# Moving the last layer's weights and first rows behind the cache pages of the last two sample batches

## What is computed

```
k_past = cache_k[page_table]          # 8 batches x 8 pages x (128 positions, 8 heads x 128)
v_past = cache_v[page_table]
s = q k^T * SCALE - slope * dist      # two components per head
p = softmax(s);  a = p[0] - lam * p[1]
o = a v                               # the sample rows' attention output

def diff_layer(...):                  # the last layer, prompt rows and sample rows alike
    o = rmsnorm(o, subln_g) * (1.0 - lambda_init)     # per head
    y = (o * silu(z)) @ w_out
    return x + y
y = rmsnorm(x, norm_f_g)
```

## Time and profile before

| | |
|---|---|
| median of 3 runs | 3050.28 us (3046.14 to 3050.70) |
| the profiled execution's own time | 3047.47 us |
| its span | 3045.8 us |
| mean granted TensorE clock | 0.989 of full speed |
| PE busy | 2953.3 us (97%) |
| sample batches, first key transpose to the last layer's first one | 2656 to 2818 us |

### The profile page before, as it was taken

How to read it: one execution, slowest core, us unless ns; L and a number is a source line. 1 busy time by engine, 2 the same in 40 slices (tenths; PEclk the granted TensorE clock), 3 DMA queues, 4 the chain that set the end, 5 groups by cost and what they waited for, 6 DMA issues and landing times. The chain is left out here.

```text
span 3045.8 us, 45887 instructions
## 1 busy us (share of the span) xinstructions
PE 2953.3 (97%) x17416; PEld 2481.7 (81%) x17416; DVE 1583.7 (52%) x2678; ACT 1268.9 (42%) x2236; POOL 135.4 (4%) x171
## 2 busy tenths in 40 slices
PE   8999999999989999899999999989999999988998
PEld 7888888889968888788888888879999999855786
DVE  3456555554532111443443433368888888644654
ACT  4443434442221101353433432257777777633422
POOL 0000000000000000000000000100000000021321
PEclk9999999999999999999999999989999999999999
DMA  7433443344344221455555455662444444399453
GB/s 259 148 137 103 141 142 124 115 147 148 119 131 154 96 97 69 155 197 187 190 186 190 158 175 184 178 158 63 103 110 103 105 108 100 121 417 407 166 181 104
DMA packets 271991, 470.33 MB, mean 154 GB/s; under 512 B 23785, under 2 KB 124633, under 8 KB 265529
## 3 DMA queue, kind: packets, MB, share of 16 engines
q1 hardware_dynamic: 269761, 467.73, 47.6%
q0 software_dynamic: 2048, 0.14, 0.0%
HBM read 357.19 MB, written 111.34 MB: 154 GB/s over the span
## 5 line engine op out<-in xcount | busy, mean ns | idle before, releaser
L1800 ACT ACTIVATE attn_scores<-attn_scores,attn_lowest 128x1024 f32<-128x1024 f32 (+15 forms) x256 | 306.8, 1203 | 10.6 <-DVE attn_lowest L1853 10.6
L1853 DVE CUSTOM_DVE_ANT_0 attn_scores<-attn_s,region_early 128x1024 f32<-128x1024 f32 (+7 forms) x256 | 216.6, 856 | 105.8 <-PE attn_s L1741 72.6
L238 PE MATMUL pool_acc<-pool_odd_x_hi,pool_wh 128*128 128x512 f32 (+1 forms) x640 | 223.2, 349 | 0.0
L240 PE MATMUL pool_acc<-pool_odd_x_hi,pool_wl 128*128 128x512 f32 (+1 forms) x640 | 222.9, 348 | 0.0
L239 PE MATMUL pool_acc<-pool_odd_x_lo,pool_wh 128*128 128x512 f32 (+1 forms) x640 | 222.9, 348 | 0.0
L238 PE MATMUL outa_acc<-outa_w_hi,outa_g_hi 128*128 128x512 f32 x512 | 201.3, 393 | 10.8 <-DVE outa_w_lo L1053 9.6
L239 PE MATMUL outa_acc<-outa_w_lo,outa_g_hi 128*128 128x512 f32 x512 | 200.1, 391 | 0.0
L238 PE MATMUL pool_acc<-even_x,pool_wh 128*128 128x512 f32 x512 | 200.1, 391 | 0.0
L240 PE MATMUL outa_acc<-outa_w_hi,outa_g_lo 128*128 128x512 f32 x512 | 199.9, 391 | 0.0
L240 PE MATMUL pool_acc<-even_x,pool_wl 128*128 128x512 f32 x512 | 199.3, 389 | 0.0
L239 PE MATMUL pool_acc<-even_x,pool_wh 128*128 128x512 f32 x512 | 199.2, 389 | 0.0
(11 more groups left out here) (282 smaller groups left out, 6668.3 us busy)
## 6 DMA issues: line engine op xcount, KB each, us to landing
pool_wz<-in_w_in_a SPq DMA_DIRECT2D x18, 2048.0 KB, 8.3
pool_wu<-w_mix SPq DMA_DIRECT2D x16, 2048.0 KB, 8.0
region_early<-in_w_kv SPq DMA_DIRECT2D x16, 2048.0 KB, 9.3
region_early<-in_w_in_b SPq DMA_DIRECT2D x16, 2048.0 KB, 8.9
hold_kq<-in_cache_k SPq DMA_DIRECT2D x64, 512.0 KB, 9.9
region_early<-in_cache_v SPq DMA_DIRECT2D x64, 512.0 KB, 9.9
region_early<-gatedT SPq DMA_DIRECT2D x16, 1024.0 KB, 5.5
gatedT<-pool_gates SPq DMA_DIRECT2D x48, 256.0 KB, 2.2
```

The lines of the kernel that those rows point to most:

```text
L238: pe.matmul(out, ah, bh, start=first, stop=False)
L240: return pe.matmul(out, al, bh, start=False, stop=last)
L1800: act.activation(part, part, ACT.Exp, scale=-1.0, bias=low[s][:, x:x + 1], accum_out=sums[s][:, i:i + 1]).then_inc(expd, 1)
L1853: dve.tensor_tensor_reduce(sc[s][:, c, a0:a0 + n], s_ps[idx % 2][:, 0:n], bias[h % 2][:, b0:b0 + n], -SCALE, low[s][:, x - 2:x - 1] if x > ...
```

## The change

The transfers that the last layer needs first are split in two groups. Before, all of them (o, z and x1 of blocks 0 and 1, the weights in four transfers of 1 MB, and the final gain, 7.5 MB together) are issued right after k(1). After, o and z of block 0 and the weights (5 MB) are issued after v(6), and o and z of block 1, x1 of both blocks and the gain (2.5 MB) after v(7). To place the first group, the last turn of SP's loop over batches is written out. On POOL, `gate(0)` moves behind the stores of batches 0 to 5, and `gate(1)` behind the store of batch 6. The streams of PE, ACT and DVE are unchanged.

```
             load_v(0, True)
             load_k(1)
-            last.first_loads(sp)
-            with sp.Fori(2, NB) as b:
+            with sp.Fori(2, NB - 1) as b:
                 load_k(b)
                 load_v(b - 1)
+            load_k(NB - 1)
+            load_v(NB - 2)
+            last.first_loads(sp)
             load_v(NB - 1)
+            last.second_loads(sp)
             last.sync(sp, sample_stored)
...
             pool.sem_inc(o_stored, FREE)
+            with pool.Fori(0, LB - 1) as b:
+                store(b)
             gate(0, 0)
+            store(LB - 1)
             gate(1, 1)
-            with pool.Fori(0, LB) as b:
-                store(b)
             gate(2, 0)
             gate(3, 1)
             store(LB)
...
     def first_loads(self, sp):
         wv = self.D["w_out_b"][0].rearrange("(k p) n -> p k n", p=P)
-        for b in range(2):
-            self.load_oz(sp, b, b)
-            self.load_x1(sp, b, b)
+        self.load_oz(sp, 0, 0)
         for j in range(self.KC // 2):
             sp.dma_start(self.w[:, 2 * j:2 * j + 2, :], wv[:, 2 * j:2 * j + 2, :]).then_inc(self.w_sem[j], 16)
+
+    def second_loads(self, sp):
+        self.load_oz(sp, 1, 1)
+        self.load_x1(sp, 0, 0)
+        self.load_x1(sp, 1, 1)
         sp.dma_start(self.gf[:, :], self.D["norm_f_g"].partition_broadcast(P)).then_inc(self.gf_in, 16)
```

## The result

The changed kernel is slower: 3056.58 us (median of 17 runs, 3053.90 to 3064.52) against 3050.28 us. The ratio of the runs to those of the kernel before is 1.0025, 95% interval 1.0019 to 1.0032, so 0.25% or 7.6 us slower by the ratio (6.3 us by the medians). Its profiled execution took 3055.36 us with a span of 3053.7 us, 7.9 us more than the span of before. The runs scatter with the clock: six of the 17 took 3059.5 to 3064.5 us at a mean granted clock of 0.983 to 0.986, the other eleven 3053.9 to 3057.6 us at 0.986 to 0.988, and the profiled execution is one of the eleven.

What follows compares the result with a forecast made beforehand. The prediction took PE to bound the kernel and DMA's backlog to pace this stage's batches. Stall +6.8 and clock +2.8 made +9.6 us on 3047.5, 3057.1; with 2.8 for the median 3059.9, stated as 3059, range 3052 to 3066.

Steps and rivals of the forecast that it cites:

- SP and DMA as two servers of nearly the same speed: Batch loads: SP issues a batch in 21.26 us, DMA does one in 20.3; before the change DMA's backlog sets the pace.
- 1.0 us from the early group's leaving: SP's queue after k(1): 11 us of freed SP time bring v(1) and k(7) forward by only 1.0 us.
- z of block 0 at 2813.7: Loads behind v(6): k(7) lands from 2792.0, block 0's z at 2813.7 (2812.5 to 2815.0).
- Who waits for it: Last batch: ACT, DVE and then PE stand until block 0's z lands; step(7) ends at 2825.0, +6.8 us.
- part 4: The step on who waits for block 0's z in the last batch, +6.8 us at the end of step(7).
- The clock, +2.8: PE after some 10 us idle in the last batch: half clock costs 2.8 us, bounds nothing and 4.4.
- Later loads at nothing: After step(7): v(7), the weights, x1 and the gain land late but are covered and cost nothing.
- the second rows as a rival: Block 1's o and z behind v(7): a 5 us slip in z's landing or gate(1) reaches PE, 3064; chance 0.13.
- a second gap in front of block 1's `last_t`: Sign of being wrong: PE waiting again before block 1's transpose in the last layer; no size given.

Runs made afterwards that it cites:

- e6: The kernel before with only SP's loop over batches written out; 3051.40 us, ratio 1.0000 against the kernel before.
- e5: The kernel of e4 with SP's loop over batches written out; 3041.57 us, ratio 0.9965 against the kernel before.
- e3: The changed kernel with o and z of block 1, x1 and the gain issued ahead of v(7); 3056.94 us, ratio 1.0021 against the kernel before.
- e1: The changed kernel with o and z of block 0 loaded right after k(1) again; 3044.70 us, ratio 0.9983 against the kernel before.
- e2: The changed kernel with ACT's and DVE's work on block 0 moved behind the last batch's key-page copies; 3051.68 us, ratio 1.0005 against the kernel before.
- e7: The kernel before with only o and z of block 0 moved behind v(6), gates as in the changed kernel; 3061.84 us, ratio 1.0032.
- e4: The changed kernel with o and z of both blocks behind k(1), gates in their old place, weights, x1 and gain between v(6) and v(7); 3046.55 us.
- e8: The kernel before with only the second group moved behind v(7) and gate(1) behind the stores; 3047.43 us, ratio 0.9988.

## Why the prediction was right

Forecast were 3059 us, slower, by a stall on block 0's z; measured were 3056.58 us, slower, by that stall.

1. **SP and DMA as two servers of nearly the same speed**: shown. e6 makes SP faster in the kernel before and gains nothing; e5 does it with the early group gone and gains 5.0 us. The changed kernel moves 397 GB/s where that of before moved 418.

2. **1.0 us from the early group's leaving**: right in kind. In the profile of the changed kernel v(1) went 2.2 us sooner, or 3.3 us counted from its own start of the stage. 2.5 us of this is the clock: the 24 transposes of step(1) took 5.38 us before, 2.84 here, and 5.38 again in all others but e5. Without it 0.8 us are left, against the 1.0 forecast. Two small misreadings cancel in that forecast: the value page is free at 2688.25 and not just before 2688.75, and from there to SP's issue inside the loop it takes 1.90 us (2689.27 to 2691.17 in e3), not the 1.15 of the written-out v(7). In e3, with the same early part as the changed kernel, k(7) is issued at 2787.24; the prediction was 2786.8, or 2787.9 with the 1.1 us by which the stage began later in both executions.

3. **z of block 0 at 2813.7**: it landed at 2812.2 in the changed kernel and at 2814.7 in e3, which is 2813.6 without the later start. The changed kernel's k(7) landed after 6.2 us, the upper bound, where I had taken 5.2.

4. **Who waits for it**: shown from both sides. ACT's gap was 15.32 us (14.05 in e3) and PE's 11.57. The prediction gave ACT's gap twice, as 2798 to 2813.7 (15.7 us) in its part 4 and as 9 to 14 us among its signs; the first was the better reading. Taking block 0's rows alone back (e1) ends it, and taking the work on it out of the copies' way (e2) ends PE's share of it; moving nothing but these rows (e7) makes it. From z's landing to the first `last_t` it took 12.25 us; forecast were 11.3 at full clock. The first `last_t` was forecast at 2825 to 2829 and started at 2824.45, in e3 at 2827.42.

5. **The clock, +2.8**: this term was mis-sized, as far as one execution shows. From 2812 to 2818 the granted clock of the changed kernel was 0.50, and it cost about 1.6 us. Pages 6 and 7 and the first piece of apply(6) ran at half speed (12 matmuls in 2.82 us, where 24 take 2.84 at full: 1.4 us; 0.86 in place of 0.64: 0.2 us), and the rest of apply(6) at full speed, 3.23 us as ever. I had taken the loss of step(1), where PE worked through from the first matmul on; here it worked in short pieces while it waited on DVE, and part of the slow time fell in those waits. No trace shows one of the six slower runs with their lower mean clock, so what the clock cost in those stays open.

6. **Later loads at nothing, and the second rows as a rival**: the weights, v(7), x1 and the gain cost nothing. The second rows cost 1.7 us in the changed kernel, a small part of the rival's 5: POOL's row of gate(1) and gate(2) ends at 2847.2, while DVE's splits end at 2842.6, so gate(2) ran beside DVE's normalisation of block 1. The rival had named another way, gate(1) itself coming too late; gate(1) ended at 2844.9, before DVE began at 2845.4. The prediction had also named a second gap in front of block 1's `last_t` as a sign of being wrong, and there is one, of 1.10 us: its "these cost nothing" fails for this part.

```profile
2837.58 9.66 POOL L2437 TENSOR_TENSOR last_z<-last_o,last_z 128x1024 f32<-128x1024 f32 x2 [10.00 <-DMA last_z<-z_rows]
```

Sum: forecast +9.6 us. e3's trace, which has step(1) at half clock as the kernel before, shows +9.2 us at the first `last_t` with 1.1 us of a later start in it, so 8.1; the changed kernel's own shows 5.1, and 7.6 with the 2.5 us of step(1) that its execution didn't lose. With 1.7 us for block 1 that makes 9.3. The measured ratio gives 7.6 us. So mechanism and place were right; the term of the clock was 1.2 us too large, block 1 was forecast at nothing and cost 1.7, and the two nearly cancel. That the numbers meet so well is in part luck. The 1.7 us between the 9.3 of the traces and the 7.6 of the runs are not explained.

That a stall and an advance lay in the same edit is what the experiments add: the early group's leaving is worth 4 to 6 us (e1, e4), and block 0's stall turns that into a loss of 6 to 8.

## What to carry to other kernels

A transfer that is moved later must be checked against the first instruction that waits for it, and then against what is queued behind that instruction on its engine: 1 MB of rows that were needed first cost 10 us, while 6.5 MB that were needed last could move with a gain. Before a queue of loads is thinned, ask which is slower, the engine that issues or those that transfer; the time from issue to landing says it (here 14.2 us falling to 8.7 while the transfers were behind, and steady at 4.7 to 5.1 while the issuer was). Removing the backlog makes the issuer the limit, and then writing out its loop, worthless before, is worth 5 us.

## What the runs showed of the hardware

The clock's half stages aren't tied to the kernel alone: after the same gap of 3.07 us in step(1), two of the ten profiled executions that are shown here (the changed kernel and e5) did the 24 transposes in 2.84 us and the others in 5.38. That is 2.5 us between executions with the same instructions there, nearly the half-width of the intervals in the table (0.0009, 2.7 us). Short waits do it too, and as irregularly: PE waited 0.43 to 0.66 us for each of three value pages in a row in step(6) of e1, e2, e3, e4 and e8, and the 16 products of the scores behind them took 3.43 to 3.51 us in e1, e3 and e4, but 1.90 in e2 and e8.

DVE can be the one that is held up by POOL: its normalisation of block 1, a product of two inputs in SBUF, took 2.90 us while POOL's gate(2) ran, and 1.23 us in e3 where it didn't. In the kernel before it was POOL that lost, 9.30 us against 2.36. The Trainium skill says both: DVE instructions with two SBUF inputs and GpSimd ones that read SBUF shut each other out, and the order of issue decides who waits ("SBUF — State Buffer", Who interferes with whom). The traces agree, with 1.7 us and 6.9 us. It need not be all or nothing for a row of instructions: in e7 and e8 the gates ran in 2.4 to 3.5 us, and the seven splits took 3.1 and 4.3 us longer.
